# Sliding-window attention in a two-layer decoder trunk: softmax on one folded 128x128 square per head

## What is computed

```
s = einsum('...qhgd,...shd->...hgqs', q, k) * scale      # 8 query heads, 2 key heads, 64 wide
diff = q_pos[..., :, None] - k_pos[..., None, :]
mask = (diff >= 0) & (diff < WINDOW) & (k_pos[..., None, :] >= 0)   # WINDOW = 128
s = where(mask, s, -1e30)
m = maximum(max(s, -1), sink)
p = exp(s - m)
p = p / (sum(p, -1) + exp(sink - m))
out = einsum('...hgqs,...shd->...qhgd', p, v)
```

## Time and profile before

| | |
|---|---|
| median of 3 runs | 2585.91 us (2583.14 to 2589.38) |
| the profiled execution | 2586.85 us |
| its span, first to last instruction | 2585.1 us |
| mean granted TensorE clock over the span | 0.966 |
| TensorE busy | 2416.6 us, 93% |
| VectorE busy | 1621.9 us, 63% |
| ScalarE busy | 753.4 us, 29% |
| GpSimd busy | 575.3 us, 22% |

### The profile page before, as it was taken

The page is one execution under the profiler, slowest core; times in us unless marked ns, Lnnn a source line. Parts: engine busy times, 40 slices in busy tenths (PEclk is TensorE's granted clock), DMA queues, the critical chain, the costliest instruction groups (busy, mean ns, idle before and its releaser), DMA issues.

```text
span 2585.1 us, 39049 instructions
## 1 busy us (share of the span) xinstructions
PE 2416.6 (93%) x14492; PEld 2306.4 (89%) x14492; DVE 1621.9 (63%) x2232; ACT 753.4 (29%) x1306; POOL 575.3 (22%) x252
## 2 busy tenths in 40 slices
PE   7999887899999999999999988879999999999995
PEld 7997687899999999999799758879999999999993
DVE  1579768655665656555636894875566555566566
ACT  2236534312122222212332472432221221212224
POOL 1111144311222221221131103522221121121212
PEclk9999888999999999999999998989999999999997
DMA  6211232111011111110031203301111111001101
GB/s 166 64 48 38 67 97 70 49 50 44 15 48 49 49 49 49 41 49 33 18 79 42 70 18 101 114 25 50 50 49 49 41 49 49 29 28 49 49 25 70
DMA packets 133524, 137.78 MB, mean 53 GB/s; under 512 B 25864, under 2 KB 124008, under 8 KB 133352
## 3 DMA queue, kind: packets, MB, share of 16 engines
q1 hardware_dynamic: 133424, 136.50, 17.9%
HBM read 124.94 MB, written 7.89 MB: 51 GB/s over the span
## 4 chain that ended last, share of the span: by engine, by line
issue 68%; POOL 14%; PE 9%; DVE 6%; DMA 1%; ACT 1%; POOLq 1%; SPq 0%; DVEq 0%; ACTq 0%
POOL wl L503 10%; PE ps L1350 4%; POOL wdl L518 4%; DVE stat L883 1%; PE ps L1373 1%; PE ps L1588 1%; PE ps L1390 1%; DVE stat L877 1%; DVE stat L886 1%; DVE hT L889 1%; DVE hT L880 1%; DVE xl L892 1%; PE ps L1394 1%; DMA xin<-in_x_prompt 0%; PE ps L1365 0%
## 5 line engine op out<-in xcount | busy, mean ns | idle before, releaser
L1350 PE MATMUL ps<-xh,wh 128*128 128x384 f32 (+1 forms) x2656 | 879.1, 331 | 14.7 <-POOL wl L503 13.6
L1350 PE MATMUL ps<-xh,wl 128*128 128x384 f32 (+1 forms) x2656 | 871.1, 328 | 0.0
L1350 PE MATMUL ps<-xl,wh 128*128 128x384 f32 (+1 forms) x2656 | 870.0, 328 | 0.0
L503 POOL TENSOR_TENSOR wl<-wraw,wh 128x1024 fp32r<-128x1024 f32 x166 | 428.3, 2581 | 1137.1 <-ACT wh L576 1137.1
L1350 PEld LDWEIGHTS ps<-xh,wh 128*128 128x128 f32 x2656 | 502.3, 189 | 30.3 <-issue 28.0
L1350 PEld LDWEIGHTS ps<-xl,wh 128*128 128x128 f32 x2656 | 502.3, 189 | 0.6 <-issue 0.4
L1350 PEld LDWEIGHTS ps<-xh,wl 128*128 128x128 f32 x2656 | 501.6, 189 | 0.0
L1212 DVE TENSOR_TENSOR hT<-hT,ps 128x384 f32<-128x384 f32 (+1 forms) x528 | 279.0, 532 | 299.5 <-PE ps L1350 299.2
L1350 PE MATMUL ps<-ah,wdh 128*128 128x384 f32 (+1 forms) x1056 | 347.2, 329 | 6.1 <-DVE al L1272 6.1
L1350 PE MATMUL ps<-ah,wdl 128*128 128x384 f32 (+1 forms) x1056 | 345.4, 327 | 0.0
L1350 PE MATMUL ps<-al,wdh 128*128 128x384 f32 (+1 forms) x1056 | 345.3, 327 | 0.0
(11 more groups left out here) (195 smaller groups left out, 2810.1 us busy)
## 6 DMA issues: line engine op xcount, KB each, us to landing
wraw<-in_w_up SPq DMA_DIRECT2D x44, 1024.0 KB, 8.3
wdraw<-in_w_down SPq DMA_DIRECT2D x44, 512.0 KB, 3.6
wraw<-in_w_out SPq DMA_DIRECT2D x24, 512.0 KB, 3.7
wraw<-in_w_out SPq DMA_DIRECT2D x48, 256.0 KB, 4.9
wraw<-in_w_in SPq DMA_DIRECT2D x11, 1024.0 KB, 6.2
xin<-in_x_prompt SPq DMA_DIRECT2D x8, 512.0 KB, 6.6
wraw<-in_w_in SPq DMA_DIRECT2D x16, 256.0 KB, 4.6
swq<-hT SPq DMA_DIRECT2D x64, 64.0 KB, 2.1
```

What stands on the lines that cost most here:

```text
L503: pool.tensor_tensor(wl[slot % 2][:], wraw[par_][:, :, 128 * (slot % 2):128 * (slot % 2) + 128], wh[slot % 2][:].bitcast(F32), ALU.subtrac ...
L1350: e = nc.tensor.matmul(out, lhs, rhs, start=(m == 0), stop=(m == n - 1))
```

## The change

Instead of keeping two squares of scores per head side by side under a mask, the changed kernel folds them into one: it copies the current block's scores (`current`, on ScalarE), then overwrites the strict upper triangle with the previous block's scores (a copy with a predicate, `copy_predicated`, on VectorE, with the 0/1 matrix `band`; in block 0 from a tile of -1e30, `negs`). Scale goes into the exponential and into the small operation that negates the maximum. Maximum, exponential and normalisation then run over 128 columns per head instead of 256, and there are four transposes per half instead of eight, into bank 4 + hf. The transposed probabilities are split again: ScalarE copies the whole square to the current slot of pTb (semaphore `a_ptc`), GpSimd sets what belongs to the previous block to zero there (`kept`, an affine_select, `a_pts`), and VectorE writes square times the transposed band to the previous slot (`previous`, `a_ptm`). `values` waits for both.

The order on VectorE changes: `softmax_in` of block b + 1 moves into block b, behind `softmax_out`, half by half after `previous`. Sb gets a second buffer, taken in turn by the blocks. On ScalarE `current(b + 1, 0)` stands ahead of the transposed copies and `current(b + 1, 1)` behind them. The constants at the start are five loads instead of four, 128 KB for the two bands instead of 384 KB for the mask.

```diff
@@ -195,7 +197,7 @@
...
-        Sb = at("Sb", [P, HEADS, 2 * P], f_off)
+        Sb = at("Sb", [P, 2, HEADS, P], f_off)
...
@@ -264,6 +266,10 @@
+
+        def heads_of(x, hf):
+
+            return x.rearrange("p (k f j) q -> p k f j q", k=2, f=2)[:, :, hf]
...
@@ -294,7 +300,7 @@
...
-            for dst, src in ((ident[:], c_ident), (mask[:], c_mask), (smask[:], c_smask), (selS[0:HEADS, :], c_sel)):
+            for dst, src in ((ident[:], c_ident), (band[:], c_band), (bandT[:], c_bandT), (smask[:], c_smask), (selS[0:HEADS, :], c_sel)):
...
@@ -533,7 +540,24 @@
 
                 pool.affine_select(out=Wt[:], in_=Wt[:], compare_op=ALU.is_ge, fill=0.0, base=0,
                                    pattern=[[0, HEADS], [1, P]], channel_multiplier=-1).then_inc(S["wt_ok"], 1)
-                for j in range(5, UP0):
+                for j in range(5, 12):
+                    lo(l, j, j % 4)
+
+                def kept(b, hf):
+
+                    k = 2 * (l * NB + b) + hf
+                    pool.wait_ge(S["a_ptc"], BEFORE + k + 1)
+                    turn(pool)
+                    keep = heads_of(pTb[:, b % 2], hf)
+                    pool.affine_select(out=keep, in_=keep, compare_op=ALU.is_ge, fill=0.0, base=0,
+                                       pattern=[[0, 2], [0, 2], [1, P]], channel_multiplier=-1).then_inc(S["a_pts"], 1)
+                for b in range(NB):
+                    for u in range(ZAT[b], ZAT[b + 1]):
+                        if u % 3 == 2:
+                            lo(l, 12 + u // 3, (12 + u // 3) % 4)
+                    kept(b, 0)
+                    kept(b, 1)
+                for j in range(16, UP0):
                     lo(l, j, j % 4)
                 lo(l, UP0, UP0 % 4)
                 lo(l, UP0 + 1, (UP0 + 1) % 4)
@@ -690,6 +714,16 @@
...
 
+                def current(b, hf):
+
+                    k = 2 * (l * NB + b) + hf
+                    act.wait_ge(S["pe_s"], BEFORE + k + 1)
+                    act.wait_ge(S["pe_tr"], BEFORE + (k - 3 if b >= 2 else 2 * l * NB))
+                    src = ps[:, 2:4, :].rearrange("p b (h s k) -> p (b h) s k", s=2, k=P)[:, :, b % 2, :]
+                    act.activation(Sb[:, b % 2, 4 * hf:4 * hf + 4, :], src, ACT.Copy).then_inc(S["a_cur"], 1)
+
+                current(0, 0)
+                current(0, 1)
                 for b in range(NB):
                     n = l * NB + b
...
@@ -697,19 +731,20 @@
                             o_evac(b - 1)
                         act.wait_ge(S["a_neg"], 2 * n + hf + 1)
                         for h in range(4 * hf, 4 * hf + 4):
-                            act.activation(Sb[:, h, :], Sb[:, h, :], ACT.Exp, bias=ast[:, 1, h:h + 1],
+                            act.activation(Sb[:, b % 2, h, :], Sb[:, b % 2, h, :], ACT.Exp, bias=ast[:, 1, h:h + 1], scale=SCALE,
                                            accum_out=ast[:, 3, h:h + 1])
                         act.activation(ast[:, 4, 4 * hf:4 * hf + 4], ast[:, 2, 4 * hf:4 * hf + 4], ACT.Exp).then_inc(S["a_exp"], 1)
                     for u in range(ZAT[b], ZAT[b + 1]):
                         zu_evac(u)
                     act.wait_ge(S["pe_pv"], BEFORE + n)
+                    if b < NB - 1:
+                        current(b + 1, 0)
                     for hf in range(2):
-                        for sl in range(2):
-                            k = 4 * n + 2 * hf + sl
-                            act.wait_ge(S["pe_tr"], BEFORE + k + 1)
-                            src = ps[:, 4 + sl, :].rearrange("p (k c) -> p k c", k=2)
-                            dst = pTb[:, sl, :, :].rearrange("p (k f j) q -> p k f (j q)", k=2, f=2)[:, :, hf, :]
-                            act.activation(dst, src, ACT.Copy).then_inc(S["a_ptev"], 1)
+                        act.wait_ge(S["pe_tr"], BEFORE + 2 * n + hf + 1)
+                        src = ps[:, 4 + hf, :].rearrange("p (k j q) -> p k j q", k=2, j=2)
+                        act.activation(heads_of(pTb[:, b % 2], hf), src, ACT.Copy).then_inc(S["a_ptc"], 1)
+                    if b < NB - 1:
+                        current(b + 1, 1)
                     if b in (2, 6):
                         zu_gelu(b // 4)
                 m_hi(l, 0)
...
                     n, hs = l * NB + b, slice(4 * hf, 4 * hf + 4)
                     k = 2 * n + hf
-                    dve.wait_ge(S["pe_s"], BEFORE + k + 1)
-                    dve.wait_ge(S["pe_tr"], BEFORE + (2 * k - 2 if b else 4 * n))
-                    dve.scalar_tensor_tensor(out=Sb[:, hs, :], in0=ps[:, 2:4, :].rearrange("p b (h k) -> p (b h) k", k=2 * P),
-                                             scalar=SCALE, in1=mask[:, b % 2 if b else 2, :].unsqueeze(1).to_broadcast([P, 4, 2 * P]),
-                                             op0=ALU.mult, op1=ALU.add).then_inc(S["a_sm"], 1)
+                    dve.wait_ge(S["a_cur"], k + 1)
+                    turn(dve)
+                    if b:
+                        prev = ps[:, 2:4, :].rearrange("p b (h s k) -> p (b h) s k", s=2, k=P)[:, :, 1 - b % 2, :]
+                    else:
+                        prev = negs[:].unsqueeze(1).to_broadcast([P, 4, P])
+                    dve.copy_predicated(Sb[:, b % 2, hs, :], band[:].bitcast(mybir.dt.uint32).unsqueeze(1).to_broadcast([P, 4, P]), prev)\
+                        .then_inc(S["a_sm"], 1)
                     dve.wait_ge(S["a_sm"], BEFORE + k + 1)
-                    dve.tensor_reduce(out=ast[:, 0, hs], in_=Sb[:, hs, :], op=ALU.max, axis=AX.X).then_inc(S["a_max"], 1)
+                    dve.tensor_reduce(out=ast[:, 0, hs], in_=Sb[:, b % 2, hs, :], op=ALU.max, axis=AX.X).then_inc(S["a_max"], 1)
                     dve.wait_ge(S["a_max"], k + 1)
 
-                    dve.scalar_tensor_tensor(out=ast[:, 1, hs], in0=ast[:, 0, hs], scalar=-1.0, in1=nsink[:, hs],
+                    dve.scalar_tensor_tensor(out=ast[:, 1, hs], in0=ast[:, 0, hs], scalar=-SCALE, in1=nsink[:, hs],
                                              op0=ALU.mult, op1=ALU.min).then_inc(S["a_m"], 1)
                     dve.wait_ge(S["a_m"], k + 1)
                     dve.tensor_tensor(ast[:, 2, hs], ast[:, 1, hs], sinkb[:, hs], ALU.add).then_inc(S["a_neg"], 1)
...
-                    dve.tensor_tensor(Sb[:, hs, :], Sb[:, hs, :], ast[:, 5, hs].unsqueeze(2).to_broadcast([P, 4, 2 * P]), ALU.mult)\
+                    dve.tensor_tensor(Sb[:, b % 2, hs, :], Sb[:, b % 2, hs, :], ast[:, 5, hs].unsqueeze(2).to_broadcast([P, 4, P]), ALU.mult)\
                         .then_inc(S["a_nrm"], 1)
+                def previous(b, hf):
+
+                    k = 2 * (l * NB + b) + hf
+                    dve.wait_ge(S["a_ptc"], BEFORE + k + 1)
+                    src = ps[:, 4 + hf, :].rearrange("p (k j q) -> p k j q", k=2, j=2)
+                    dve.tensor_tensor(heads_of(pTb[:, 1 - b % 2], hf), src,
+                                      bandT[:].unsqueeze(1).unsqueeze(1).to_broadcast([P, 2, 2, P]), ALU.mult).then_inc(S["a_ptm"], 1)
@@ -1042,10 +1088,11 @@
...
                 pre(0)
+                dve.wait_ge(S["pad_ok"], 3)
+                softmax_in(0, 0)
+                softmax_in(0, 1)
                 for b in range(NB):
                     n = l * NB + b
-                    softmax_in(b, 0)
-                    softmax_in(b, 1)
...
                     softmax_out(b, 1)
+                    for hf in range(2):
+                        previous(b, hf)
+                        if b < NB - 1:
+                            softmax_in(b + 1, hf)
                 dve.wait_ge(S["kv_tr"], l + 1)
...
@@ -1481,17 +1532,17 @@
 
                 def turned(b, hf):
                     pe.wait_ge(S["a_nrm"], 2 * (l * NB + b) + hf + 1)
-                    for sl in range(2):
-                        k = 4 * (l * NB + b) + 2 * hf + sl
-
-                        pe.wait_ge(S["a_ptev"], BEFORE + (k - 1 if b or hf else 4 * l * NB))
-                        for i in range(4):
-                            e = pe.transpose(ps[:, 4 + sl, P * i:P * i + P], Sb[:, 4 * hf + i, P * sl:P * sl + P], ident[:])
-                        e.then_inc(S["pe_tr"], 1)
+                    k = 2 * (l * NB + b) + hf
+                    for n in ("a_ptc", "a_ptm"):
+                        pe.wait_ge(S[n], BEFORE + (k - 1 if b else 2 * l * NB))
+                    for i in range(4):
+                        e = pe.transpose(ps[:, 4 + hf, P * i:P * i + P], Sb[:, b % 2, 4 * hf + i, :], ident[:])
+                    e.then_inc(S["pe_tr"], 1)
 
                 def values(b):
                     n = l * NB + b
-                    pe.wait_ge(S["a_ptev"], BEFORE + 4 * n + 4)
+                    pe.wait_ge(S["a_ptm"], BEFORE + 2 * n + 2)
+                    pe.wait_ge(S["a_pts"], 2 * n + 2)
                     pe.wait_ge(S["a_vr"], BEFORE + n + 1)
                     pe.wait_ge(S["a_oev"], BEFORE + n)
                     for kv in range(KV):
```

(12 more changed lines are left out.)

18 lines of the change are left out of this document (10 added, 8 removed).

## The result

The changed kernel took 2591.74 us (median of 20 runs, 2583.32 to 2596.57) beside 2583.48 for the kernel before (20 runs, 2572.31 to 2592.56): a ratio of 1.0032, 95% interval 1.0022 to 1.0042, so **slower by 0.32%, some 8 us**. Forecast were 2582, a gain of 3.9 on the 2585.91 known then, and "no change" as the likeliest outcome. The range, 2571 to 2598, holds the time; the likeliest case's own range, 2577 to 2586, doesn't. The profiled execution of the changed kernel took 2592.5 us for a span of 2590.7.

A forecast was written before the change was run, and what follows sets the result against it. Bound: the attention stage's dependence chain, TensorE and VectorE both near full. Per layer -1.7 (blocks 0 to 6), -0.3 (block 7), +0.15 (start); -3.7 in all from 2586.85 gives 2583.1, less 0.94: 2582 us, range 2571 to 2598.

The forecast's parts named there:

- the likeliest case: The forecast's own chain of dependences holds, whole program at 2577 to 2586 us; chance 0.50.
- The chain from S to V: Per attention block, from issuing the next block's first-half scores (S) to issuing this block's values (V): 5.6 us, before 4.55.
- The copy with a predicate: VectorE's overwrite of the scores' upper triangle, 512 elements: taken at 0.69 us, upper bound 1.22.
- GpSimd's select: Zeroing the previous block's entries, 0.55 us per half, upper bound 1.09; covered by the chain, so costed at zero.
- The stalls: Normalisation waits vanish behind one z_u unit; block 3's values issue 1.0 us late; block 7 takes 12.4 us, before 12.7.
- The sum for the chain: Per layer, block 0's first-half scores issue to block 6's values issue: 84.8 us after, 86.5 before, so -1.7.
- S0 to V6: The stretch from block 0's S to block 6's V in one layer's attention stage, forecast at 84.8 us.
- the clock falls in every block: Rival: new idling halves TensorE's clock in 5 more blocks per layer, 17 us slower, 2599; chance 0.13.
- VectorE as the bound: Rival: the stage follows VectorE's relief of 1.8 us in four blocks per layer, 14 us faster, 2571; chance 0.20.
- The longer chain: Rival: a predicated copy at 1.22 us, or longer hops, adds 0.53 per block, 8.5 us, 2590; chance 0.17.
- Everything outside the stage unmoved: Sign of being right: the program outside the attention stages keeps its times.
- The exclusive lock: GpSimd's selects could hold up VectorE's small L1021 or L1024; 15 us if each hit, counted as none.

The follow-up runs named there:

- a2_after: The changed kernel run again with no edit; 2587.53 us, ratio 1.0025 to the kernel before.
- e1_fill: The changed kernel plus useless identity transposes in TensorE's idle time, nine before the second scores, three before the values; 2587.00 us, ratio 1.0014 to the kernel before.
- e6_pad: The changed kernel plus one unused tile of 1,536 bytes per partition, putting later tiles at their old addresses; 2590.32 us, ratio 1.0026 to the kernel before.
- e3_fold_first: The changed kernel with VectorE's predicated copy for the next block's first half ahead of both `previous`, maxima after; 2565.80 us, ratio 0.9933 to the kernel before.
- e2_noselect: The changed kernel without GpSimd's select, values waiting for ScalarE's copy instead (computes something else); 2590.02 us, ratio 1.0032 to the kernel before.

## Why the prediction was wrong, point by point

- **The chain from S to V: right.** 5.6 forecast, 5.48 measured in blocks 0, 1, 2 and 5; 5.75 in block 4.
- **The copy with a predicate: right in kind,** 0.69 taken, 0.725 measured; the upper bound of 1.22 was far off. Exponentials at 0.39: 0.390.
- **GpSimd's select: right but for blocks 6 and 7,** 0.55 taken, 0.636 measured. In block 6 the selects end at S + 5.0, as counted, but on their way they hold up L1059 and with it V by 0.37 us, where the forecast had said "still covered"; in block 7 the values wait for the select, 0.18 us. In all 0.4 us.
- **The stalls: right.** No wait for the normalisation in blocks 1 and 6. Block 3's V was put 1.0 late and came 0.4 to 1.5 late (V - S 5.86 to 6.99 over three profiles); block 7 was put at 12.4 and took 12.35.
- **The sum for the chain: right.** 84.8 forecast for S0 to V6; 84.79 in the layer of a2_after whose blocks had no fall, 84.88 in both layers of e1_fill.
- **The step that failed is TensorE's clock.** The sum left it at full speed, and the rival "the clock falls in every block" was given 0.13 because both falls of the kernel before stood beside one unbroken wait of 2.4 us or more, "and the new waits are 1.5 and 0.8 with 1.1 of work between". The new waits came as said, 1.61 and 0.58, and the clock fell beside them: 3 and 4 blocks in the two layers of one profile, none and 3 in the other, 0.8 to 1.7 us each. The rival's mechanism and its price (0.9 to 2 us each) were right; its count of 10 falls was too high and its chance too low. The falls turn -3.2 us (e1_fill's stages, where -3.7 was forecast) into +1.7 to +6.7, 4.7 on average, in three profiles of the changed order, e6_pad's among them. That is some 8 of the 12 us between the forecast change and the measured one. The rest is the residue outside the stages, below. The Trainium skill (TensorE: Matmul & The Clock Gate, "A second HAM failure mode: psum-queue depth-cycling") says that frequent short idling between groups of matmuls makes the clock oscillate; here row and page agree in kind, and the prediction had cited it and then weighed two rows of another pattern above it. Two falls beside long waits say that long waits suffice; they don't say that short ones don't.
- **VectorE as the bound: wrong,** as the chain argument against it said. VectorE's 23 us of relief in the stage went into idling before the chain (3.12 us in block 0). e3_fold_first shows that with the same volume the order alone is worth 26 us against the changed kernel.
- **The longer chain: not what happened.** No link was longer than counted but L1059 in block 6.
- **"Everything outside the stage unmoved": not quite.** The changed kernels carry about 3 us (1.1 to 6.8) that their stages don't show. TensorE spends more time at the lower level there; what brings that about is open, and nothing points to the addresses of the tiles.
- **The exclusive lock** (SBUF — State Buffer, "Who interferes with whom" in the Trainium skill) reached the new selects in one block per layer. As counted, they end before L1059 and L1062 start in most blocks, and both take 0.16. In block 6, behind the weight split, the second select and L1059 meet, and L1059 (two inputs in SBUF) takes 0.54 until the select ends; without the select it takes 0.17. By that rule one of the two has to wait, and the trace agrees. The forecast had placed those selects at 3.8 to 5.0 and L1059 at 4.4, and didn't put the two side by side. The largest case in the same trace is L1237, at 2.36 us instead of 0.28 beside a weight split.

## What to carry to other kernels

Taking work off an engine that waits moves nothing by itself: write out the chain with its start and end times, and ask of each instruction on the serving engine whether the waiting one needs it before or after its neighbour. Here the saving in volume gave +0.3%, and the same instructions in another order gave -0.7%. When a change turns one long wait of TensorE into several short ones, price the clock as well: count the blocks that would idle in pieces and put a real chance on each falling, and test it with idle-time filler, which changes the clock and leaves the chain alone.

## What the runs showed of the hardware that was not expected

- Pieces of idling of 1.61 and 0.58 us with 1.1 us of matmuls between them can bring TensorE from 2.4 to 1.2 GHz (values 3.52 us instead of 1.94), and with identical waits it happens in one execution and not in another. With one piece of 0.63 (e1_fill) or 0.54 (e3_fold_first) a block, blocks 0 to 2 showed none in either layer, though neither did they with both pieces in a2_after.
- A copy with a predicate over 128x512 costs 0.725 us with its data in PSUM and 0.737 with them in SBUF (4 of them), 5 to 7% above a plain operation of that shape (0.69).
- GpSimd's triangular select costs 0.636 us for 512 elements and 1.094 for 1,024: not quite in proportion.
- A VectorE operation on 128x4 with two inputs in SBUF took 0.54 us instead of 0.16 beside a select of GpSimd that reads SBUF, and ended with it, in block 6 of both layers; with the select left out (e2_noselect) it took 0.17.
- A weight split on GpSimd took 3.20 us instead of 2.34 where a VectorE operation with two inputs in SBUF was under way at its start, and the small VectorE operation behind it 2.36 instead of 0.28. Seen, not tested by a run.
